# A two-layer hybrid trunk: the first k, gates and first v of each layer multiplied together tile by tile, and the low parts of the weights shared between two engines by stage

## The reference, cut to what matters

```python
h = rms_norm(x, norm_g) * (1.0 + scale[:, None]) + shift[:, None]
(conv_val, conv_glu, conv_z, dq, dk, dv, dz, dbeta, ddecay,
 aq, ak, av, az, mgate) = jnp.split(h @ w_in, IN_SPLITS, axis=-1)
...
qkv = jax.nn.silu(depthwise_conv(jnp.concatenate([q, k, v], axis=-1), dn_conv_w))
...                                  # gated delta rule in both directions, 4 heads
beta = jax.nn.sigmoid(beta_logit); g = -jnp.exp(dn_a_log) * jax.nn.softplus(decay_logit + dn_dt_bias)
...                                  # differential attention, 4 heads; conv module with layer norm
y = jnp.stack(ys, axis=2)            # the three branches, 512 wide each
gates = jax.nn.sigmoid(gate_logits)
x_new = x + gate[:, None] * (jnp.sum(gates * jnp.einsum('btnw,nwd->btnd', y, w_branch), axis=2) @ w_out)
```

## Time and profile before

| | us |
|---|---|
| runs: lowest, median, highest | 2035.63, 2039.96, 2040.71 |
| the profiled execution, its own time | 2030.62 |
| its span (first to last instruction) | 2028.8 |
| TensorE busy with matmuls | 1824.2 (90% of the span) |
| VectorE busy | 1083.1 (53%) |
| ScalarE busy | 973.9 (48%) |
| GpSimd busy | 856.8 (42%) |

### The profile page before, as it was taken

The page is one execution under the profiler, slowest core; times in us unless marked ns, Lnnn a source line. Parts: engine busy times, 40 slices in busy tenths (PEclk is TensorE's granted clock), DMA queues, the critical chain, the costliest instruction groups (busy, mean ns, idle before and its releaser), DMA issues. The chain is left out here.

```text
span 2028.8 us, 27795 instructions
## 1 busy us (share of the span) xinstructions
PE 1824.2 (90%) x11060; PEld 1511.9 (75%) x11060; DVE 1083.1 (53%) x1536; ACT 973.9 (48%) x1300; POOL 856.8 (42%) x638
## 2 busy tenths in 40 slices
PE   6879996899998999979898977989799999898989
PEld 5767886888887777757687865868697777776767
DVE  4646493569566464644113144658759956365122
ACT  6557524345353454533454145664327455454651
POOL 1132434646544434333277212334245634333483
PEclk9989997999999999979899988999799999999999
DMA  7113223421221222212234312233312222112343
GB/s 285 45 60 105 74 81 124 143 63 52 73 73 52 77 72 70 86 50 94 91 109 138 115 63 76 79 89 109 90 60 77 73 63 68 52 63 71 101 134 126
DMA packets 76415, 178.87 MB, mean 88 GB/s; under 512 B 6464, under 2 KB 29312, under 8 KB 76160
## 3 DMA queue, kind: packets, MB, share of 16 engines
q1 hardware_dynamic: 34272, 122.46, 19.3%
q10 hardware_dynamic: 42016, 54.63, 8.0%
HBM read 156.00 MB, written 21.07 MB: 87 GB/s over the span
## 5 line engine op out<-in xcount | busy, mean ns | idle before, releaser
L1879 POOL TENSOR_TENSOR wLs<-raw,wHs 128x512 fp32r<-128x512 f32 x420 | 606.1, 1467 | 788.5 <-ACT wHs L830 788.5
L465 PE MATMUL banks<-hH,wHs 128*128 128x512 f32 x1984 | 602.8, 366 | 58.3 <-DVE hL L433 19.3
L465 PE MATMUL banks<-hL,wHs 128*128 128x512 f32 x1984 | 583.6, 356 | 0.0
L465 PE MATMUL banks<-hH,wLs 128*128 128x512 f32 x1984 | 583.2, 356 | 0.0
L465 PEld LDWEIGHTS banks<-hH,wHs 128*128 128x128 f32 x1984 | 328.7, 193 | 134.5 <-issue 26.6
L465 PEld LDWEIGHTS banks<-hL,wHs 128*128 128x128 f32 x1984 | 327.4, 192 | 56.6 <-issue 2.9
L465 PEld LDWEIGHTS banks<-hH,wLs 128*128 128x128 f32 x1984 | 326.4, 192 | 55.0
L830 ACT ACTIVATE wHs<-raw 128x1024 fp32r<-128x1024 f32 x210 | 220.2, 1053 | 252.6 <-DMA raw<-wstream 252.3
L1449 DVE SCALAR_TENSOR_TENSOR acc<-padc,vecs,acc 128x783 f32<-128x783 f32 (+1 forms) x240 | 300.3, 1305 | 0.0
L819 ACT ACT_TABLE_LOAD x183 | 234.8, 1283 | 30.3 <-issue 12.8
L864 ACT ACTIVATE Pa<-banks,stat 128x768 f32<-128x768 f32 (+1 forms) x80 | 64.5, 812 | 117.0 <-DVE stat L1409 115.7
(11 more groups left out here) (241 smaller groups left out, 2404.2 us busy)
## 6 DMA issues: line engine op xcount, KB each, us to landing
raw<-wstream SPq DMA_DIRECT2D x210, 512.0 KB, 3.6
araw<-wstream SPq DMA_DIRECT2D x16, 512.0 KB, 12.4
E<-g_rows ACTq DMA_DIRECT2D x16, 384.0 KB, 6.7
egb<-eg_rows ACTq DMA_DIRECT2D x20, 256.0 KB, 4.0
inb<-intra_rows ACTq DMA_DIRECT2D x20, 256.0 KB, 4.3
parked_logits<-sg ACTq DMA_DIRECT2D x13, 384.0 KB, 4.1
xs<-xT SPq DMA_DIRECT2D x8, 384.0 KB, 11.3
intra_rows<-E ACTq DMA_DIRECT2D x8, 384.0 KB, 3.1
```

The lines of the kernel that those rows point to most:

```text
L465: last = pe.matmul(out[:, a:b], w, m[:, kt, a:b], start=(kt == 0 and j == 0), stop=(kt == kts - 1 and j == 2))
L1879: ins = pool.tensor_tensor(wL[w % RING][:, o:o + 512], raw[w % RING][:, o:o + 512], wH[w % RING][:, o:o + 512].bitcast(F32), ALU.subtract)
```

## The change

The order at the start of a layer becomes `nh`, `dk0`, `gb`, `dv0`, `dq0`; `gturn` comes behind `dk1`, and `vt` and `dsum` of head 0 behind `dv1`, with the first `decay` behind those. On TensorE, `dk0`, `gb` and `dv0` are computed together: for each tile of x all three units are multiplied, when that tile is there. The low parts of the kinds in `low_on_vector` (33 units a layer and the last eight `ada` units of layer 0, 74 of 210) are made on VectorE in one instruction of 128 x 1024 each, at the places where `low` is called: an item's call covers units up to two behind its own. The fourth unit of a layer (`dq0`) is made right behind the last `hL`. GpSimd skips these units.

```diff
@@ -98,16 +98,15 @@
     for l in range(DEPTH):
-        out += [("nh", l), ("gb", l)]
-        for h in range(NT):
-            out.append(("dqkv", l, h, "dk"))
-            out += [("vt", l, h - 1), ("dsum", l, h - 1)] * (h > 0)
-            out += [("dsil", l, h, "dk"), ("dqkv", l, h, "dv"), ("dsil", l, h, "dv")]
-            out += [("gturn", l)] * (h == 0)
-            out.append(("dqkv", l, h, "dq"))
-            out += [("dturn", l, h - 1)] * (h > 0) + [("dsil", l, h, "dq"), ("dsq", l, h)]
-            out += [("kq", l, h - 1)] * (h > 0)
-            out.append(("decay", l, h))
+        out += [("nh", l), ("dqkv", l, 0, "dk"), ("gb", l), ("dqkv", l, 0, "dv"), ("dsil", l, 0, "dk"),
+                ("dsil", l, 0, "dv"), ("dqkv", l, 0, "dq"), ("dsil", l, 0, "dq"), ("dsq", l, 0)]
+        for h in range(1, NT):
+            last = [("vt", l, h - 1), ("dsum", l, h - 1)]
+            out += [("dqkv", l, h, "dk")] + ([("gturn", l)] if h == 1 else last)
+            out += [("dsil", l, h, "dk"), ("dqkv", l, h, "dv")] + last * (h == 1) + [("dsil", l, h, "dv")]
+            out += [("decay", l, 0)] * (h == 1)
+            out += [("dqkv", l, h, "dq"), ("dturn", l, h - 1), ("dsil", l, h, "dq"), ("dsq", l, h)]
+            out += [("kq", l, h - 1), ("decay", l, h)]
         glu = [("glu", l, t) for t in range(NT)]
@@ -173,6 +172,11 @@
+def low_on_vector(u):
+
+    return u[0] in ("gb", "dk", "dv", "dq", "cz", "branch2", "branch0", "wout") or u[0] == "ada" and u[1] == 0
+
+
 FIRST = [("ada", 0, m) for m in range(2 * KT)]
@@ -468,8 +472,27 @@
                 out = product(pe, u, ntok(u[1], kind))
-                last = dense(u, out, hH, hL, segs(ntok(u[1], kind)), KT, dep=("h", u[1]) if kind == "gb" else None)
+                last = dense(u, out, hH, hL, segs(ntok(u[1], kind)), KT)
                 last.then_inc(*tick("pe", "pe", u))
+
+            def three_by_tile(l):
+
+                three = [("dk", l, 0), ("gb", l, 0), ("dv", l, 0)]
+                outs = [product(pe, u, TOK) for u in three]
+                for u in three:
+                    pe.wait_ge(*done("hi", u))
+                    pe.wait_ge(*done("lo", u))
+                for kt in range(KT):
+                    pe.wait_ge(*done("h", l, kt))
+                    cc = slice(kt * P, kt * P + P)
+                    for u, out in zip(three, outs):
+                        i = WIDX[u] % RING
+                        for j, (w, m) in enumerate(((wH[i], hH), (wH[i], hL), (wL[i], hH))):
+                            for a, b in segs(TOK):
+                                last = pe.matmul(out[:, a:b], w[:, cc], m[:, kt, a:b], start=(kt == 0 and j == 0),
+                                                 stop=(kt == KT - 1 and j == 2))
+                        if kt == KT - 1:
+                            last.then_inc(*tick("pe", "pe", u))
@@ -581,8 +604,6 @@
                         held.clear()
-                elif k == "gb":
-                    unit(units_of(it)[0], "gb")
                 elif k == "gturn":
@@ -598,7 +619,10 @@
                     h, kind = it[2], it[3]
-                    unit((kind, l, h), kind)
+                    if h == 0 and kind == "dk":
+                        three_by_tile(l)
+                    elif h or kind == "dq":
+                        unit((kind, l, h), kind)
                 elif k == "vt":
@@ -1426,6 +1450,20 @@
             added = set()
+            done_lo = [0]
+
+            def low(u, n):
+
+                while done_lo[0] < min(WIDX[u] + n, len(UNITS)):
+                    w = done_lo[0]
+                    v = UNITS[w]
+                    done_lo[0] += 1
+                    if not low_on_vector(v):
+                        continue
+                    dve.wait_ge(*done("hi", v))
+                    dve.tensor_tensor(wL[w % RING][:, :], raw[w % RING][:, :], wH[w % RING][:, :].bitcast(F32),
+                                      ALU.subtract).then_inc(*tick("dve", "lo", v))
+
             last_gm = [None, None]
@@ -1483,6 +1521,10 @@
                             dve.tensor_scalar(nlam[:, v:v + 1], nlam[:, v:v + 1], -lam0, None, ALU.add).then_inc(*tick("dve", "nlam", v))
+                    if l == 0 and m == 6:
+                        low(UNITS[0], RING - 1)
+                    for u in units_of(it):
+                        low(u, RING - 1)
                     if m:
@@ -1494,6 +1536,7 @@
                 elif k == "nh":
+                    low(("dk", l, 0), RING - 1)
                     dve.wait_ge(*done("gs", l))
@@ -1508,7 +1551,9 @@
                     lowh(l, KT - 1)
+                    low(("dk", l, 0), RING)
                 elif k == "gb":
+                    low(units_of(it)[0], RING - 1)
                     dve.wait_ge(*done("gln", l))
@@ -1542,6 +1587,7 @@
                     W = TOK + 1 if n == TOK else SEQ
+                    low((kind, l, h), RING - 1)
                     w0 = V_DW + 3 * (NT * ("dq", "dk", "dv").index(kind) + h)
@@ -1734,6 +1780,8 @@
                     n = ntok(l, "glu")
+                    low(("val", l, t), RING - 1)
+                    low(("glu", l, t), RING - 1)
                     dve.wait_ge(*done("read", ("glu", l, t), 0))
@@ -1747,6 +1795,7 @@
                     n = ntok(l, "gate")
+                    low(("branch%d" % n_, l, p), RING - 1)
                     for j in range(2):
@@ -1768,7 +1817,10 @@
                 elif k in ("gate", "qunit", "vunit"):
+                    low(units_of(it)[0], RING - 1)
                     conv(l, 1)
+                elif k in ("park", "leafpark", "z"):
+                    low(units_of(it)[0], RING - 1)
                 elif k == "lnsum":
@@ -1835,6 +1887,7 @@
                     n = ntok(l, "az")
+                    low(("az", l, h), RING - 1)
                     dve.wait_ge(*done("aors", l, h))
@@ -1874,6 +1928,8 @@
                     done_lo[0] += 1
+                    if low_on_vector(v):
+                        continue
                     pool.wait_ge(*done("hi", v))
```

## The result

The changed kernel took 2011.8 us (median of four runs, 2005.1 to 2016.2), the kernel before beside it 2038.2 us: ratio 0.9868, 95% interval [0.9836, 0.9899]. That is 26.4 us less, where I had forecast about 14 and given 2014 as the low end of the range. The direction was right, the size was not.

The account below looks back on a forecast made before the run. TensorE, busy for 90% of the span, was taken as the bound, with only idle time and slow stretches to win. Terms 1 + 4 + 1.4 + 7.6 + 0.8 - 1.5 + 0.8 = 14.1 us gave 2025.5 us, range 2014 to 2037.

Parts of the forecast that it names:

- Part 2: Head stage: what the joint product and new order move; 1 us won in layer 0, 4 us in layer 1.
- 1 us won in layer 0: Head stage, layer 0: dv3 starts at 192.6 instead of 193.65; bounds 2 us lost to 3 won.
- 4 us won in layer 1: Head stage, layer 1: dv3 at 1327.4 instead of 1330.13, plus 1.4 us of clock; bounds -1 and 5.
- 1.4 us of clock behind `dv3`: Layer 1: dv3 also starts at full clock, winning 1.4 us, part of that layer's 4 us.
- VectorE's first sum took 2.10 us beside GpSimd's low part and 1.02 alone: Head loop: without GpSimd's low part a head is 1.1 us shorter, until TensorE's own work is the bound.
- ScalarE's stretch from the exponentials to `dv1` out of PSUM: Layer 0: ScalarE's copies, silus, table loads, DMA issues and waits take 27 us, from 103.3 to 130.3, releasing dq1.
- the squares only as a bound: Layer 0's lower bound: 2 us lost if GpSimd's squares meet head 0's convolutions, each costing 1.1 us.
- 4.0 us earlier: Start of layer 0: the joint product of gb, dk0 and dv0 ends at 83.8 instead of 87.79.
- First `branch0` product of layer 1: Its wait shrinks as GpSimd's round loses both low parts: 7.6 us won (4 to 8).
- contention eats the gain: Rival, chance 0.18: VectorE's low parts meet GpSimd's work, the 8.4 us of branch0 fall away: 2034.
- Start of `out`: Third wout unit's low part stands ahead of the first hL: 1.5 us lost in layer 0, 0.8 won in layer 1.
- Late `ada` units: Layer 0: the first wait stays, the second (2.8 us) shrinks by half; 1.4 us won (0 to 2.5).

Follow-up runs that it names:

- after: The changed kernel as first measured against the kernel before: 2011.8 us, ratio 0.9868; its profiled execution took 2016.21 us.
- after_again: The changed kernel run once more, nothing altered, beside the kernel before: 2008.3 us, ratio 0.9865.
- head_low: low_only with only the head stage's units (gb, dk, dv, dq; 26 of 74) having low parts on VectorE: 2014.1 us, ratio 0.9888.
- joint_only: The changed kernel with joint product and new order, but every low part on GpSimd: 2038.3 us, ratio 1.0008.
- low_only: The changed kernel without the joint product: low parts on VectorE, units one after another in the old order: 2006.8 us, ratio 0.9855.
- dk1_early: The changed kernel with VectorE making the low part of dk1 ahead of its gate work: 2005.3 us, ratio 0.9846.
- joint_l0: dk1_late with the joint product and its order in layer 0 alone: 2000.5 us, ratio 0.982.
- dk1_late: dk1_early with the third wout unit's low part made behind the hL at the start of out: 1999.9 us, ratio 0.982.
- rest_low: low_only with the head stage's low parts back on GpSimd; late ada, cz, branch2, branch0 and wout stay on VectorE: 2025.4 us, ratio 0.9942.
- low_late: low_only with the third wout unit's low part made behind the eight hL instead of ahead of the first: 2002.5 us, ratio 0.983.

## Why the prediction was wrong

**The step that failed is the head stage, Part 2: "1 us won in layer 0" and "4 us won in layer 1".** The traces show 4.2 and 7.5 us in layer 0 (after, after_again), 8.4 and 8.6 in layer 1; head_low wins 22 us with this stage alone.

The shortfall arises in heads 0 and 1, in which I had counted no relief of VectorE's sums: `dv2` was to start at 159.7 us, "as before (159.5)", and in layer 1 "1.5 us late". It starts at 155.17, and in layer 1, counted from the layer's first product, 4.9 us early. In joint_only, which has the same order with the low parts on GpSimd, it starts at 158.99, and in layer 1 0.3 us late. So at `dv2` the forecast fits the order alone (ahead of it joint_only is earlier, `dq1` at 127.8 against 130.3), and what it left out is what the move of the low parts does to these two heads. From `dv2` to `dv3` it held: 32.9 us in layer 0 (33.9 in after, 32.1 in after_again) and 28.5 in layer 1 (28.3). The 1.4 us of clock behind `dv3` in layer 1 don't show, the lead shrinks from 9.3 to 8.4 us there.

The reading behind it was wrong as well: "On it VectorE's first sum took 2.10 us beside GpSimd's low part and 1.02 alone". The row of 2.10 us is the second sum, and it ran beside GpSimd's square (178.55 to 180.33). I took the contention from this one row and charged it once a head, from head 2 on. It is in every convolution of the kernel before, also in the scalar form (0.98 instead of 0.62).

One step is worth following. ScalarE's stretch from the exponentials to `dv1` out of PSUM I had at 27 us, from 103.3 to 130.3. It took 24.5, from 102.4 to 126.9: 3.4 of the 3.6 us by which `dv3` came earlier than forecast (189.05 against 192.6) arise up to here. ScalarE waited 3.4 us for convolutions (I had 4) and 6.1 for its DMA issues (7.1). In joint_only the stretch takes 27.2 us, with 7.0 us of waits for the slower convolutions. That my 27 fits that kernel is luck, since its parts don't.

I had also written of the squares only as a bound. With GpSimd's queue empty they come earlier: 3.4 us of wait in low_only instead of 8.1 in layer 0, 5.1 instead of 8.9 in layer 1, though its order is that of before.

**Right by position:** the joint product ends at 83.2 (83.8), the scans at 99.1 (100.0), `dk1` waits 8.7 and 12.6 us (8.7, 11.9), and ScalarE, not this wait, sets the end of the stage; dk1_early moved the wait and won 3 us of 21. **But the joint product is worth nothing:** joint_only is at 1.0008. I had made no term of it by itself, and its "4.0 us earlier" is in the sum only through head 0; yet I saw in it the main part of the change. Low parts on VectorE do the same with the units one after another (0.9855), and in layer 1 the profiles give that order more, 11.2 to 13.5 us against 8.4 to 9.9, which the medians of joint_l0 and dk1_late could not confirm.

**First `branch0` product of layer 1:** 7.6 us forecast, 7.3 to 7.4 measured up to 1960 us of before in after, after_again and rest_low; start 1939.4 with 1.7 us idle. The rival "contention eats the gain" is refuted. **Start of `out`:** a loss of 1.5 was forecast in layer 0, where idle time grew from 2.9 to 4.75 us, and a win of 0.8 in layer 1, where it grew too, from 2.9 to 3.7: that sign was wrong. low_late takes it back (3.0 and 2.1) and shows that it was the placing of one low part. **Late `ada` units:** 1.4 forecast, from 0.6 won to 0.9 lost in rest_low, after_again and after, so nothing that can be told. My 1.21 us for the new low part is 1.22 in the traces, and 2.49 where GpSimd runs.

**The step from the profile to the median.** I took the terms as equal for every execution. By the medians the change is worth 26 to 29 us, by the profiles 14.4 and 21.7. The head terms, 16.1 us in after_again instead of 5, account for 11 us of the difference to my sum. 1 to 4 us are left. The granted clock may hold them: before's profile had 0.952 against a mean of 0.948, and the changed kernel has 0.9525 in the mean. 0.0045 of 2030 us is about 9 us, more than is left, and a part of it is in the head terms already. That the changed kernel has the better clock because it has fewer idle times is my guess: no run here holds the clock fixed.

## What to carry to other kernels

When a step leaves GpSimd, look in VectorE's rows for every instruction that is 1.5 to 2 times as long in one place as in another, and add up all of them that lie on the chain; the relief may be worth more than the step itself. Where one engine's result releases work on both, as ScalarE's does here, they meet again and again. A wait that is the largest in the list can still be worth nothing if the engine behind it is late by itself: undoing it alone (one line) told this at once.

## What the runs showed that I had not expected

GpSimd's writes (three of 128x1024, 1.00 us each) left VectorE's three-operand sums at 1.02 us, while its two-operand subtractions, even of constants that nobody else touched, made them 1.94: it is GpSimd's reading that costs. The scalar form, with one input, was longer beside the writes in a few of the convolutions (1.12 us in head 1 of layer 0 instead of 0.62, 0.77 instead of 0.49 where q is 512 wide).

The same program up to `out`, run twice, differed by 6.7 us in the attention stage of layer 0, with equal busy time and a granted clock of 0.83 against 0.96 between 840 and 880 us. A single pair of profiles can't settle an effect of that size. The table shows more, and leaves it open: in attention six profiles lose 3.5 to 7.5 us and the other seven at most 1.0. The six are just those of the kernels that have both groups of low parts on VectorE and the third `wout` unit's low part early. That unit comes after the attention stage, so no run here shows how it could act there.
